# Products of 576 tokens moved as 512 and 64 columns in place of 288 and 288

## The chip, the cores and the metric

The kernel runs on one core of a Trainium2 chip. Its time is the device time of that core in microseconds. The kernel before takes 2556.81 us, the median of two runs (2554.54 and 2559.07).

## The reference

One inference step of a trunk of two layers with a model width of 1024, for 512 prompt tokens and 8 x 8 sample tokens. The kernel takes all 576 tokens through the weights together. Layer 0 has an HGRN2 mixer (a gated linear recurrence with 8 heads), layer 1 an S5 mixer (a diagonal complex state-space layer). Each mixer stands between two half-step SwiGLU feed-forward networks of inner width 2816. All is float32.

```python
def _swiglu(h, w_in, w_out):
    a, b = jnp.split(h @ w_in, 2, axis=-1)
    return (jax.nn.silu(a) * b) @ w_out

for i in range(DEPTH):                                   # DEPTH = 2
    x = x + 0.5 * _swiglu(_rmsnorm(x, ln_ffn1[i]), ffn1_w_in[i], ffn1_w_out[i])
    h = _rmsnorm(x, ln_mix[i])
    out = hgrn2(h) if i == 0 else s5(h)                  # h @ w_in (4 x 1024), ... ; z @ w_glu (2 x 1024)
    x = x + out
    x = x + 0.5 * _swiglu(_rmsnorm(x, ln_ffn2[i]), ffn2_w_in[i], ffn2_w_out[i])
```

## The kernel before

Activations lie with channels on the 128 partitions and the T = 576 tokens along the free axis. The large products run on TensorE in the type fp32r. To keep float32 accuracy each operand is split into a high and a low part, and each product is the sum of three: weights high x activations high, high x low, low x high (w_hi, w_lo; h_hi, h_lo, and likewise g, z, o). A 128x128 block of weights is the stationary operand, the tokens are the moving one.

`product` (line 1655 on) makes one output tile of 128 channels x 576 tokens. It loops over the kt blocks of input channels, over the three part products, and over two halves h of the tokens, HALF = 288 columns each; every half is one matmul, recorded on line 1672, into its own PSUM bank of 512 floats (bank 2s + h, columns 0 to 287). Both halves use the same weights block one after the other. Each matmul call brings its own weight load. Two slots s of two banks each alternate; the semaphore `full[s]` tells that a tile is finished (it is raised by the last matmul of the tile) and `free[s]` that its reader has taken it.

The phases run in order: for each feed-forward network two groups of "up" (kt = 8) and "down" (kt = 12 or 10), the HGRN input and output projections (kt = 8), and the S5 output product "glu" (kt = 8). In the HGRN phase, pieces of a product (a few k) are put between the score levels of the head before (line 1807 and its neighbours), in an order written out by hand. The S5 recurrence has no product beside it except for the first pieces of "glu".

The readers of the PSUM tiles see the two halves through `pair(s)`, a view of two banks with 288 columns each, and bring the SBUF side into the same shape with `halves`. They are `scaled` (line 1086: multiply by the norm's factor), the residual update of "down" (line 1356), and for "glu" the sigmoid on ScalarE (line 1030) and the multiplication on VectorE (line 1614). Other uses of 288-column halves (the sums over channels on lines 1655 and 1863, and the readers of lines 770, 888, 967 and 1600) are not touched. Weights come by DMA into w_raw, ScalarE makes w_hi from them (line 732) and GpSimd w_lo (line 635).

Of the kernel before, what the change touches and what calls it, by code (L numbers as in the profile page):

```python
# [20 lines left out]
ALU = mybir.AluOpType  # L21
ACT = mybir.ActivationFunctionType

D_MODEL = 1024
SEQ = 512
# [10 lines left out]
P = 128  # L36
SAMPLE = DEC_BATCH * DEC_SEQ
T = SEQ + SAMPLE
HALF = T // 2
# [79 lines left out]
def build_trunk(nc, x_prompt, x_sample, state_hgrn, state_s5_re, state_s5_im, ln_ffn1, ffn1_w_in, ffn1_w_out,  # L119
# [9 lines left out]
    def sb(name, shape, dt=F32, at=None):  # L129

        size = 1 if dt == U8 else 4
        for n in shape[1:]:
            size *= n
        size += -size % 32
        where = place["at"] if at is None else at
        if at is None:
            place["at"] += size
        assert where + size <= limit, (name, where + size, limit)
        return nc.alloc_sbuf_tensor_at(name, shape, dt, offset=where)

    x = sb("x", [P, NK, T])
# [6 lines left out]
    rstd = sb("rstd", [P, T])  # L148
# [20 lines left out]
    t_a = sb("t_a", [P, T])  # L169
    t_b = sb("t_b", [P, T])  # L170
    t_s = sb("t_s", [P, T])
# [91 lines left out]
    ps = nc.alloc_psum_tensor("ps", [P, 8, BANK], F32)  # L263
# [9 lines left out]
    def sem(name):  # L273
        return ctx.enter_context(nc.semaphore(name))

    with ctx:
# [13 lines left out]
        free = [sem(f"free{s}") for s in range(2)]  # L290
# [99 lines left out]
        up_at, at = {}, 0  # L390
# [18 lines left out]
        def cols(t, i, n=1):  # L409

            flat = t[:].rearrange("p a b -> p (a b)")
            w = t.shape[2]
            return flat[:, bass.ds(i * w, n * w)]

        def halves(ap):
            return ap.rearrange("p (h t) -> p h t", h=2)

        def pair(s):
            return ps[:, 2 * s:2 * s + 2, 0:HALF]

        def f32(ap):
            return ap.bitcast(F32)

        def lifted(ap):

            return ap.rearrange("p (n t) -> p t n", t=LIFT)
# [280 lines left out]
        def _(act):  # L707
# [26 lines left out]
            def split_next(n, ph, j, i, last):  # L734

                if j == 0:
                    if isinstance(i, int) and i == 0:

                        if n and ph.kind != "hgrn_out":
                            split(ph, 1, 0, PH[n - 1], None)  # L740
                    else:
                        split(ph, 1, i, ph, i - 1)
                elif not last:
                    split(ph, 0, i + 1, ph, i)
                elif n + 1 < len(PH) and (ph.kind, ph.name) not in MAKES:
                    split(PH[n + 1], 0, 0, ph, None)

            def split_ahead(n, ph, j, last):

                if last and j == 0 and n + 1 < len(PH) and (ph.kind, ph.name) in MAKES:  # L750
                    split(PH[n + 1], 0, 0, ph, None)
# [184 lines left out]
            def s5(n, ph):  # L936
# [3 lines left out]
                for q in range(2):  # L940
                    v = ps[:, 6, 2 * P * q:2 * P * (q + 1)].rearrange("p (b s) -> p b s", s=ST)
                    ins = nc.scalar.activation(s5_s[:, q, :, PROMPT_BLOCKS:].rearrange("p s b -> p b s"), v, ACT.Copy)
# [7 lines left out]
                for at in range(NK + 2):  # L950
                    if at < NK:
# [5 lines left out]
                        for h in range(2):  # L957
                            v = ps[0:BLOCKS, h, :].rearrange("n (t g c) -> n t g c", g=G_CT, c=GROUP_CH)
                            ins = nc.scalar.activation(o[:, 4 * h:4 * h + 4], v, ACT.Copy)
# [65 lines left out]
                def unit(i, j, last=False):  # L1025
                    split_next(n, ph, j, i, last)
                    t = i * 2 + (ph.tile0 + j)
                    act.wait_ge(full[1], t + 1)
                    act.wait_ge(gs_done, i * 2 + j)
                    nc.scalar.activation(halves(t_s[:]), pair(1), ACT.Sigmoid).then_inc(free[1], 1)  # L1030
                    split_ahead(n, ph, j, last)
                    norm_tile(5, i * 2 + j, (gs_done, i * 2 + (j + 1)))

                for j in range(2):
                    unit(0, j)
# [6 lines left out]
            for n, ph in enumerate(PH):  # L1042
# [4 lines left out]
                                 scale=1.0 / D_MODEL, bias=eps_t[0:SAMPLE]).then_inc(rms_root, 1)  # L1047
# [10 lines left out]
        def _(dve):  # L1058
            link = Chain(dve, dve_link)
            V = nc.vector  # L1060
# [12 lines left out]
            def clear_ssq(r):  # L1073
                if r:
                    dve.wait_ge(norm_full, r)
                V.memset(ssq[:], 0.0).then_inc(ssq_zero, 1)
                dve.wait_ge(ssq_zero, r + 1)
# [5 lines left out]

            def scaled(dst, s):

                return V.tensor_tensor(halves(dst), pair(s), halves(rstd[:]), ALU.mult)  # L1086


            clear_ssq(0)
            for m in range(NK + 1):  # L1090
                if m < NK:
                    b = 4 + 2 * (m % 2)
# [248 lines left out]
            def down(ph):  # L1341
                r = MAKES.get((ph.kind, ph.name))
                pieces = ph.kind == "down" and ph.name[0] == "ffn1_0"
                if r is not None:
                    if ph.kind == "hgrn_out":
                        dve.wait_ge(o_ready, HEADS)
                    clear_ssq(r)
                scale = 1.0 if ph.kind == "hgrn_out" else 0.5

                def unit(i, j):  # L1350
                    if pieces and j == 0:
                        b_part(i + ph.name[1] * (NK // 2))
                        c_part(i + ph.name[1] * (NK // 2))
                    m = i * 2 + j
                    dve.wait_ge(full[j], i + (ph.tile0 + 1))
                    V.scalar_tensor_tensor(out=halves(cols(x, m)), in0=pair(j), scalar=scale, in1=halves(cols(x, m)),  # L1356
                                           op0=ALU.mult, op1=ALU.add).then_inc(free[j], 1)
                    if r is not None:
                        norm_tile(r, m)

                link.settle()
                at, per = link.base, 6 + 2 + 5 + 5 if pieces else 0
                if pieces:
                    for j in range(2):
                        unit(0, j)
                    assert link.n == per
                    link.n = 0
                with dve.Fori(int(pieces), ph.pairs) as i:
                    link.base = i * per + at
                    for j in range(2):  # L1370
                        unit(i, j)
                    assert link.n == per
                    link.n = 0
                link.base = at + ph.pairs * per
# [163 lines left out]
            def s5(ph):  # L1538
                reciprocal(4)
                for ct in range(NK):  # L1540
                    V.scalar_tensor_tensor(out=u_t[:, ct].rearrange("p (t n) -> p t n", t=LIFT), in0=lifted(x[:, ct]),
                                           scalar=vec[:, NORMS[4][0] + ct:NORMS[4][0] + ct + 1], in1=lifted(rstd[:]),
# [52 lines left out]
                for ct in range(NK):  # L1595

                    dve.wait_ge(t3_full, ct + 1)
                    if ct >= 2:
                        dve.wait_ge(gelu_done, ct - 1)
                    V.scalar_tensor_tensor(out=halves(y_f[ct % 2][:]), in0=halves(u_t[:, ct]),  # L1600
                                           scalar=vec[:, COL["s5_d"] + ct:COL["s5_d"] + ct + 1],
                                           in1=pair(1), op0=ALU.mult, op1=ALU.add).then_inc(yy_done, 1)
# [6 lines left out]
                def unit(i, j):  # L1609
                    t = i * 2 + (ph.tile0 + j)  # L1610
                    m = i * 2 + j
                    dve.wait_ge(full[0], t + 1)
                    dve.wait_ge(free[1], t + 1)
                    V.tensor_tensor(halves(t_a[:]), pair(0), halves(t_s[:]), ALU.mult).then_inc(free[0], 1)
                    dve.wait_ge(free[0], t + 1)
                    V.tensor_tensor(cols(x, m), cols(x, m), t_a[:], ALU.add).then_inc(gs_done, 1)
                    norm_tile(5, m)
# [19 lines left out]
        def _(pe):  # L1637
            M = nc.tensor

            def turn(out, t, n=P, w=P):  # L1640

                return M.transpose(out, t, ident[0:n, 0:n])  # L1642
# [15 lines left out]
            def product(ph, j, a, i, hi, lo, before=None, part=None):  # L1658


                k0, k1 = part or (0, ph.kt)
                s, t = (a, i * 2 + (ph.tile0 + j)) if ph.cols == 2 else (j, i + ph.tile0)
                if k0 == 0:
                    pe.wait_ge(w_ready[j], i + (ph.pair0 + 1))
                    pe.wait_ge(free[s], t)
                for k in range(k0, k1):
                    if before is not None:
                        before(k)
                    at = (a * ph.kt + k) * P
                    for n, (w, v) in enumerate(((w_hi, hi), (w_hi, lo), (w_lo, hi))):  # L1670
                        for h in range(2):
                            ins = M.matmul(ps[:, 2 * s + h, 0:HALF], w[j][:, at:at + P], v[:, k, h * HALF:(h + 1) * HALF],  # L1672
                                           start=k == 0 and n == 0, stop=k == ph.kt - 1 and n == 2)
                if k1 == ph.kt:
                    ins.then_inc(full[s], 1)
# [363 lines left out]
            for c in range(CHUNKS + 1):  # L2039
# [13 lines left out]
                for k in range(NK):  # L2053
                    ins = turn(ps[0:n, Y_BANK[c] + k // 4, (k % 4) * P:(k % 4 + 1) * P], y_n[:, k, c * P:c * P + n])
# [29 lines left out]
```

## Time and profile before

| | |
|---|---|
| two runs | 2554.54 and 2559.07 us |
| median | 2556.81 us |
| span of the profiled execution (no other time is given for it) | 2558.5 us |
| instructions | 42966 |
| TensorE busy | 2370.1 us (93%) |
| TensorE weight loads busy | 2321.2 us (91%) |
| VectorE, ScalarE, GpSimd busy | 1001.8, 664.1, 782.2 us |
| DMA | 211.04 MB, 82 GB/s on average |
| mean granted TensorE clock | 0.961 of full |

Busy times are unions of the instructions' records. A record of a matmul lasts from its start to its modelled end and contains the time in which the result runs through the array, so that consecutive records overlap: how fast they follow each other is read from their starts, or from the number of records in a stretch. An f32 matmul shows as two records, an fp32r matmul as one.

### The profile page before, as it was taken

The numbers are of one execution on the slowest core, as the hardware profiler recorded it, in microseconds if no ns is written. First come the engines' busy times: TensorE is split into PE (matmuls) and PEld (weight loads), VectorE is DVE, ScalarE is ACT, GpSimd is POOL, SyncE is SP. The second block draws the span as 40 slices with busy tenths as digits, with TensorE's granted clock in tenths as the row PEclk, the third lists the DMA queues.
The fourth block names the chain that finished last, engine by engine and source line by source line (L and its number), as shares of the span: only waits on it lengthen the run. The fifth ranks groups of instructions, "written<-read, shape, count | busy, mean of one in ns | idle before, by whom it ended". The sixth has DMA issues, their size and how long they took to land.

```text
span 2558.5 us, 42966 instructions
## 1 busy us (share of the span) xinstructions
PE 2370.1 (93%) x17438; PEld 2321.2 (91%) x17438; DVE 1001.8 (39%) x1538; ACT 664.1 (26%) x750; POOL 782.2 (31%) x223
## 2 busy tenths in 40 slices
PE   6989999998888888999999999999982899999998
PEld 5989999888788877999999999999972899999998
DVE  5845523756665663321122322112259323211222
ACT  3222222332222212322122322122241532221223
POOL 2332333222212212333333333333320133333332
PEclk9999999999898997999999999999986899999999
DMA  4223422441113102432332322232242333223212
GB/s 121 66 61 110 129 82 62 125 112 51 51 50 84 50 17 68 124 90 74 105 102 68 97 82 74 77 96 76 72 136 66 88 82 83 82 70 94 82 58 78
DMA packets 398491, 211.04 MB, mean 82 GB/s; under 512 B 23025, under 2 KB 393922, under 8 KB 398402
## 3 DMA queue, kind: packets, MB, share of 16 engines
q1 hardware_dynamic: 387666, 198.03, 27.9%
q10 hardware_dynamic: 10736, 11.77, 1.4%
q8 instruction: 63, 1.03, 0.2%
q14 instruction: 26, 0.21, 0.0%
HBM read 193.01 MB, written 20.94 MB: 84 GB/s over the span
## 4 chain that ended last, share of the span: by engine, by line
PE 57%; DVE 2%; issue 1%; ACT 1%; POOL 0%; DMA 0%; SPq 0%; DVEq 0%; ACTq 0%
PE ps L1672 55%; PE ps L1642 1%; PE ps L1971 0%; PE ps L1972 0%; DVE sq L1558 0%; DVE sq L1555 0%; DVE ssq L1556 0%; PE ps L1945 0%; POOL w_lo L635 0%; DMA wc<-wc_d 0%; DVE z_lo L1592 0%; DVE s_s L1559 0%; PE ps L1655 0%; DVE s_e L1559 0%; SPq L514 0%
## 5 line engine op out<-in xcount | busy, mean ns | idle before, releaser
L635 POOL TENSOR_TENSOR w_lo<-w_raw,w_hi 128x2048 fp32r<-128x2048 f32 (+3 forms) x184 | 741.6, 4030 | 1584.3 <-ACT w_hi L732 1584.3
L1672 PE MATMUL ps<-h_hi,w_hi 128*128 128x288 f32 x3328 | 731.6, 302 | 17.9 <-DVE t_a L1086 15.6
L1672 PE MATMUL ps<-h_lo,w_hi 128*128 128x288 f32 x3328 | 720.3, 298 | 0.0
L1672 PE MATMUL ps<-h_hi,w_lo 128*128 128x288 f32 x3328 | 719.7, 298 | 0.0
L1672 PEld LDWEIGHTS ps<-h_hi,w_hi 128*128 128x128 f32 x3328 | 544.0, 192 | 23.6 <-DVE t_a L1086 12.7
L1672 PEld LDWEIGHTS ps<-h_lo,w_hi 128*128 128x128 f32 x3328 | 544.1, 191 | 0.0
L1672 PEld LDWEIGHTS ps<-h_hi,w_lo 128*128 128x128 f32 x3328 | 543.7, 191 | 0.0
L732 ACT ACTIVATE w_hi<-w_raw 128x2048 fp32r<-128x2048 f32 (+3 forms) x184 | 309.5, 1682 | 216.5 <-PE ps L1672 204.2
L1672 PE MATMUL ps<-g_hi,w_hi 128*128 128x288 f32 x1408 | 304.7, 298 | 1.4 <-POOL w_lo L635 1.4
L1672 PE MATMUL ps<-g_lo,w_hi 128*128 128x288 f32 x1408 | 302.9, 297 | 0.0
L1672 PE MATMUL ps<-g_hi,w_lo 128*128 128x288 f32 x1408 | 302.7, 297 | 0.0
L1086 DVE TENSOR_TENSOR t_b<-ps,rstd 128x576 f32<-128x576 f32 x88 | 66.6, 757 | 447.2 <-PE ps L1672 447.2
L1672 PEld LDWEIGHTS ps<-g_hi,w_hi 128*128 128x128 f32 x1408 | 228.3, 190 | 1.8 <-issue 1.8
L1672 PEld LDWEIGHTS ps<-g_lo,w_hi 128*128 128x128 f32 x1408 | 228.5, 190 | 0.0
L1672 PEld LDWEIGHTS ps<-g_hi,w_lo 128*128 128x128 f32 x1408 | 228.2, 190 | 0.0
L798 ACT ACTIVATE g_hi<-t_g 128x576 f32 (+1 forms) x88 | 60.4, 686 | 539.7 <-DVE t_g L1314 539.7
L1356 DVE SCALAR_TENSOR_TENSOR x<-ps,x 128x576 f32 (+1 forms) x72 | 54.4, 756 | 360.4 <-PE ps L1672 360.4
L1086 DVE TENSOR_TENSOR t_a<-ps,rstd 128x576 f32<-128x576 f32 x88 | 66.7, 758 | 252.2 <-PE ps L1672 251.3
L795 ACT ACTIVATE t_s<-t_a 128x576 f32<-128x576 f32 x88 | 60.4, 686 | 322.9 <-DVE t_a L1086 322.9
L1807 PE MATMUL ps<-q_t,k_t 128*128 128x128 f32 x512 | 76.3, 297 | 44.3 <-DVE e_t L1403 35.0
L1807 PEld LDWEIGHTS ps<-q_t,k_t 128*128 128x128 f32 x512 | 69.5, 208 | 48.0 <-DVE e_t L1403 37.0
L1316 DVE TENSOR_TENSOR g_lo<-t_g,g_hi 128x576 f32 (+1 forms) x88 | 66.7, 758 | 82.1 <-ACT g_hi L798 82.1
(301 smaller groups left out, 1975.3 us busy)
## 6 DMA issues: line engine op xcount, KB each, us to landing
w_raw<-in_ffn_w_in_dram SPq DMA_DIRECT2D x176, 512.0 KB, 4.9
w_raw<-in_ffn_w_out_dram SPq DMA_DIRECT2D x64, 384.0 KB, 3.7
w_raw<-in_ffn_w_out_dram SPq DMA_DIRECT2D x64, 320.0 KB, 3.4
w_raw<-in_hgrn_w_in_dram SPq DMA_DIRECT2D x32, 512.0 KB, 5.3
w_raw<-in_s_w_glu_dram SPq DMA_DIRECT2D x16, 512.0 KB, 4.7
wb_d<-wb_st ACTq DMA_DIRECT2D x8, 512.0 KB, 2.8
wc_d<-c_pow ACTq DMA_DIRECT2D x8, 512.0 KB, 3.5
s_in<-in_state_hgrn_dram SPq DMA_DIRECT2D x8, 512.0 KB, 4.0
```

The lines of the kernel that those rows point to most:

```text
L635: nc.gpsimd.tensor_tensor(w_lo[j][:, 0:n], w_raw[j][:, 0:n], f32(w_hi[j][:, 0:n]), ALU.subtract)\
L732: nc.scalar.activation(w_hi[j][:, 0:ph.size], w_raw[j][:, 0:ph.size], ACT.Copy).then_inc(w_hi_done[j], 1)
L795: nc.scalar.activation(t_s[:], t_a[:], ACT.Silu).then_inc(silu_done, 1)
L798: nc.scalar.activation(cols(g_hi, i * 2 + j), t_g[:], ACT.Copy).then_inc(g_hi_done, 1)
L1086: return V.tensor_tensor(halves(dst), pair(s), halves(rstd[:]), ALU.mult)
L1316: V.tensor_tensor(cols(g_lo, i * 2 + j), t_g[:], f32(cols(g_hi, i * 2 + j)), ALU.subtract)\
L1356: V.scalar_tensor_tensor(out=halves(cols(x, m)), in0=pair(j), scalar=scale, in1=halves(cols(x, m)), op0=ALU.mult, op1=ALU.add).then_inc(fr ...
L1642: return M.transpose(out, t, ident[0:n, 0:n])
L1672: ins = M.matmul(ps[:, 2 * s + h, 0:HALF], w[j][:, at:at + P], v[:, k, h * HALF:(h + 1) * HALF], start=k == 0 and n == 0, stop=k == ph.kt ...
L1807: ins = M.matmul(ps[:, 4 + n % 2, at], k_t[b][:, at], q_t[b][:, at], start=True, stop=True)
```

## The change

Line 1672 moves tokens 0 to 511 in one matmul of 512 columns, which fills bank 2s, and tokens 512 to 575 in one of 64 columns into the start of bank 2s + 1. The number of matmuls and of weight loads, their order and their semaphores stay. A tile then lies contiguous over the two banks, and a new view `both(s)` gives its 576 columns in one piece to the four readers, which read and write plain 576-element rows (the fifth edited place is the new view itself).

```diff
@@ -418,6 +418,10 @@
         def pair(s):
             return ps[:, 2 * s:2 * s + 2, 0:HALF]
 
+        def both(s):
+
+            return ps[:, 2 * s:2 * s + 2, :].rearrange("p b t -> p (b t)")[:, 0:T]
+
@@ -1027,7 +1031,7 @@
-                    nc.scalar.activation(halves(t_s[:]), pair(1), ACT.Sigmoid).then_inc(free[1], 1)
+                    nc.scalar.activation(t_s[:], both(1), ACT.Sigmoid).then_inc(free[1], 1)
@@ -1083,7 +1087,7 @@
-                return V.tensor_tensor(halves(dst), pair(s), halves(rstd[:]), ALU.mult)
+                return V.tensor_tensor(dst, both(s), rstd[:], ALU.mult)
@@ -1353,7 +1357,7 @@
-                    V.scalar_tensor_tensor(out=halves(cols(x, m)), in0=pair(j), scalar=scale, in1=halves(cols(x, m)),
+                    V.scalar_tensor_tensor(out=cols(x, m), in0=both(j), scalar=scale, in1=cols(x, m),
                                            op0=ALU.mult, op1=ALU.add).then_inc(free[j], 1)
@@ -1611,7 +1615,7 @@
-                    V.tensor_tensor(halves(t_a[:]), pair(0), halves(t_s[:]), ALU.mult).then_inc(free[0], 1)
+                    V.tensor_tensor(t_a[:], both(0), t_s[:], ALU.mult).then_inc(free[0], 1)
@@ -1668,8 +1672,8 @@
                     for n, (w, v) in enumerate(((w_hi, hi), (w_hi, lo), (w_lo, hi))):
-                        for h in range(2):
-                            ins = M.matmul(ps[:, 2 * s + h, 0:HALF], w[j][:, at:at + P], v[:, k, h * HALF:(h + 1) * HALF],
+                        for h, (t0, t1) in enumerate(((0, SEQ), (SEQ, T))):
+                            ins = M.matmul(ps[:, 2 * s + h, 0:t1 - t0], w[j][:, at:at + P], v[:, k, t0:t1],
                                            start=k == 0 and n == 0, stop=k == ph.kt - 1 and n == 2)
```

## Rows read from the trace of the kernel before

**Rows 1.** The page: engines (busy us, share, instructions) and the granted clock in 40 slices.

```profile
PE 2370.1 (93%) x17438; PEld 2321.2 (91%) x17438; DVE 1001.8 (39%) x1538; ACT 664.1 (26%) x750; POOL 782.2 (31%) x223
...
PEclk9999999999898997999999999999986899999999
```

**Rows 2.** TensorE's waits: who for whom, us in total, times, longest.

```profile
PE ps L1807 <- DVE e_t L1403: 35.0, 9, 4.7
PE ps L1807 <- DVE q_t L1386: 9.3, 7, 2.5
PE ps L1672 <- DVE z_lo L1592: 5.0, 6, 2.0
```

**Rows 3.** Stretches: length, busy us (xcount) by engine, clock, DMA; the first, line 1672 alone.

```profile
540.00:1000.00 460.00, 256.31 (x1618) 237.04 (x1618) 0.90 0.18 51
...
1200.00:1300.00 100.00, 100.00 (x753) 100.00 (x752) 12.61 (x17) 18.33 (x14) 35.87 (x9) 1.00 0.38 104
1860.00:2010.00 150.00, 88.82 (x836) 82.80 (x835) 104.06 (x208) 59.82 (x101) 15.31 (x10) 0.78 0.38 109
```

**Rows 4.** Groups of TensorE on line 1672, one of three: xcount, busy us, mean ns.

```profile
L1672 PE MATMUL ps<-h_hi,w_hi 128*128 128x288 f32 x3328 | 731.6, 302 | 17.9 <-DVE t_a L1086 15.6 <-issue 2.0 <-POOL w_lo L635 0.3
...
L1672 PE MATMUL ps<-g_hi,w_hi 128*128 128x288 f32 x1408 | 304.7, 298 | 1.4 <-POOL w_lo L635 1.4
...
L1672 PE MATMUL ps<-z_hi,w_hi 128*128 128x288 f32 x256 | 56.7, 304 | 5.9 <-DVE z_lo L1592 5.0 <-ACT t_s L1030 0.8
...
L1672 PE MATMUL ps<-o_hi,w_hi 128*128 128x288 f32 x128 | 31.4, 330 | 9.0 <-DVE o_lo L1474 4.6 <-POOL w_lo L635 4.4
```

**Rows 5.** Timeline of TensorE, 8-column products: start us, us, instruction.

```profile
660.49 1.95 PE L1856 MATMUL ps<-q_t,s_in 128*128 128x8 f32 x16
```

**Rows 6.** Timeline of TensorE, 128-column products, and the record lengths of their neighbours.

```profile
653.89 1.05 PE L1834 MATMUL ps<-v_tok,k_tok 128*128 128x128 f32 x8
...
L1834 PE MATMUL ps<-v_tok,k_tok 128*128 128x128 f32 x64 | 9.5, 295 | 0.8 <-ACT k_tok L879 0.8
```

**Rows 7.** Records of loads, and the 8-column product: duration ns min/median/max.

```profile
L1672 PEld LDWEIGHTS ps<-h_hi,w_hi x3328: 186/188/338, 27.2 to 2479.1; 128*128 128x128 f32 x196
...
L1856 PEld LDWEIGHTS ps<-q_t,s_in x128: 186/192/333, 606.6 to 970.3; 128*128 128x128 f32 x128
L1856 PE MATMUL ps<-q_t,s_in x128: 256/256/380, 606.6 to 970.4; 128*128 128x8 f32 x128
```

**Rows 8.** Timeline of the weight loads and products of line 1842, 512 columns.

```profile
656.46 0.29 PEld L1842 LDWEIGHTS ps<-v_seq,k_tok 64*128 64x128 f32 x2 [0.17 <-issue]
657.00 0.19 PEld L1842 LDWEIGHTS ps<-v_seq,k_tok 64*128 64x128 f32 x1 [0.24 <-issue]
657.43 0.19 PEld L1842 LDWEIGHTS ps<-v_seq,k_tok 64*128 64x128 f32 x1 [0.24 <-issue]
...
656.46 1.98 PE L1842 MATMUL ps<-v_seq,k_tok 64*128 64x512 f32 x4
```

**Rows 9.** Timeline of TensorE at the half clock.

```profile
861.49 0.68 PE L1672 MATMUL ps<-h_hi,w_lo 128*128 128x288 f32 x2
861.97 0.68 PE L1672 MATMUL ps<-h_hi,w_hi 128*128 128x288 f32 x2
```

**Rows 10.** Timeline of TensorE, f32 products of 288 columns, and their record length.

```profile
1035.15 1.13 PE L1655 MATMUL ps<-ssq,ones 128*128 128x288 f32 x4
...
L1655 PE MATMUL ps<-ssq,ones x24: 404/406/511, 41.4 to 2126.9; 128*128 128x288 f32 x24
```

**Rows 11.** The page, groups: a reader of PSUM and the making of w_lo.

```profile
L1086 DVE TENSOR_TENSOR t_b<-ps,rstd 128x576 f32<-128x576 f32 x88 | 66.6, 757 | 447.2 <-PE ps L1672 447.2
...
L635 POOL TENSOR_TENSOR w_lo<-w_raw,w_hi 128x2048 fp32r<-128x2048 f32 (+3 forms) x184 | 741.6, 4030 | 1584.3 <-ACT w_hi L732 1584.3
```

## Prediction

> **What bounds the kernel now.** I read the page's busy times first: TensorE is busy 93% of the span and its weight loads 91%, at a granted clock that is full in most slices [rows 1]. Then the waits of TensorE: the longest is 35.0 us in total [rows 2], so hardly anything but its own stream holds it. Then the stretches: from 1200 to 1300 us it issues 753 products and is never idle, while VectorE is busy 12.61 us of 100 [rows 3]. The groups of instructions say which stream that is. Line 1672 has 3 x (3328 + 1408 + 256 + 128) = 15,360 matmuls of 288 columns, 7,680 pairs [rows 4]. Per pair the dense stretch gives 2 x 100 / 753 = 0.2656 us, so 7,680 pairs are 2,040 us of the 2,558.5 us span. This change touches exactly that stream: whatever a pair gains or loses lies on the path that sets the end.
>
> **What a matmul is made of.** Every matmul, the second with the same weights too, has a weight load of its own: 753 loads and products in the dense stretch [rows 3]. What the load takes has to be read from stretches where the product is too short to hide it. The 8-column products of line 1856 carry 128x128 weights: sixteen last 1.95 us of which the last's own record is 0.256, so they follow at (1.95 - 0.256) / 15 = 0.113 us [rows 5], though 8 columns are next to no work. The eight 128-column products of line 1834 follow at (1.05 - 0.295) / 7 = 0.108 us [rows 6]. So one load costs 0.108 to 0.113 us however short its product is. That those are f32 and ours fp32r makes no difference in the load's record: 188 ns for line 1672, 192 for line 1856 [rows 7].
> How far ahead can a load run? Line 1842 has 512 columns in each record: the third and fourth loads start at 657.00 and 657.43, one product apart, after 0.24 us in which the load side stood idle [rows 8]. So with 0.43 us of room, loads do not run two ahead: the next starts when the product before it does. A pair of 288s hides both loads (two products of 0.133 against loads of 0.11). In 512 + 64 the load for the 64 hides under the 512, but the load for the next 512 can start only with the 64, whose columns are over long before.
>
> **The change, part by part.**
> *The 512-column product.* At the half clock the 288 columns take 0.24 us (two products from 861.49 to 861.97) [rows 9], one column per cycle of 1.2 GHz, so at 2.4 GHz they are 0.120 and the 0.1328 measured holds 0.0128 more. 512 columns are 0.2133. Lower bound: the 288-column f32 products of line 1655 follow at (1.13 - 0.406) / 3 = 0.241 us, twice 0.120 and about 0.001 more [rows 10], so the excess might vanish: 0.215. Upper bound: the excess grows with the columns, 0.1328 x 512 / 288 = 0.236. I take it as a fixed sum per product, 0.226, the middle between them.
> *The 64-column product.* 64 columns are 0.027 us, the load behind it 0.108 to 0.113. The load decides; I take 0.113, as the 8-column rows are nearest to a short product.
> *The pair.* 0.226 + 0.113 = 0.339 us in place of 0.2656: +0.0734. Bounds 0.323 and 0.349: +0.057 and +0.083. Over 7,680 pairs: **+564 us**, bounds +440 and +641.
> *Pairs at the half clock.* From 540 to 1000 us, 1,618 matmuls of line 1672 are busy 256.3 us [rows 3] against 1,618 x 0.1328 = 215; of the 41 us over, I put 15 to the tails of separate pieces (9 steps of some 10 pieces by the code, 0.16 us each), so 26 / 0.107, about 240 matmuls or 120 pairs, ran at 1.2 GHz. There the pair would go from 0.480 to 0.427 + 0.217 (twice the fast load) = 0.644, 0.09 more than the 0.073 counted: +10 us.
> *Waits that a slower TensorE fills.* In the HGRN stage the products lie between the score levels; a longer piece covers the 9.3 us for VectorE's q_t [rows 2] and perhaps the few us for z_lo in the S5 stage. The 35.0 us for e_t are 9 waits; a piece of three k ahead of each is 9 pairs and grows by 0.7 us, so some 6 us go and the rest stays. Together -18 us.
> *The five readers of PSUM.* They read the same 576 elements, contiguous rather than two times 288; VectorE's take 757 ns and have 447.2 us of idle time behind TensorE [rows 11]. Cost nothing; if a record became 50 ns longer or shorter, only the last of each stage would reach the end, under 1 us. No queue, wait, DMA or semaphore moves. Weight supply gets more time: GpSimd's 184 groups busy 741.6 us, behind ScalarE 1584.3 us idle [rows 11].
> **Sum:** 564 + 10 - 18 = +556. The page gives no time of its own for the profiled execution beyond the span, 2558.5; it lies between the two runs (2554.54 and 2559.07), 1.7 above their median 2556.81. 2556.81 + 556 = **3113 us**, 22% slower.
>
> **Rivals.**
> *Two loads ahead, or the second load of the same weights for nothing.* Then the 64 costs its columns and one overhead, 0.028 to 0.040, and the pair 0.243 to 0.266: between -0.0226 x 7,680 = -174 us and no change; its middle 0.255 gives -82, 2475 us. It decides from the point at which the short product's cost falls under 0.040. For it: nothing in the rows shows fp32r loads behind a short fp32r product. Against: rows 5 and 8. By the Trainium skill, "TensorE: Matmul & The Clock Gate", section "Back-to-back issue gap", 512 columns are 518 cycles and 1 to 64 columns about 60; a pair would be 578 / 2.4 = 241 ns, and the time about 2370, faster. The trace speaks against that table for streams with a weight load each (8 columns: 113 ns, not 25), and its 134 cycles (56 ns) for 128 columns aren't met either (108 ns). Chance 0.03: two thirds faster, one third within 2%.
> *Load and short product one after the other.* If the load for the next 512 began only once the 64 columns are through, 0.027 is added: +205, 3325 us. For it: 0.113 against 0.108 could be that. Against: the 128-column products at 0.108, whose columns alone take nearly that, leave no room for a load in series [rows 6]. Or fp32r could run narrow products at a slower rate; up to four cycles a column (the rate of the two f32 records) 64 columns are 0.107 and still hidden by the load, so it costs only in series, +0.107 x 7,680 = +820. Chance 0.07, mostly near 3325.
> *The narrow product is taken in two passes as f32 is.* Two records with a load each: +0.113 more, +868, 3990 us. The f32 groups show such doubling (line 1842: four records for two products) [rows 8], fp32r at 288 columns none. Chance 0.03.
> *The clock falls.* TensorE's columns fill 0.240 of 0.339 us, 71%, in place of 90%. In the S5 stretch it was busy 89 of 150 us and the granted clock 0.78 [rows 3], but with idle stretches in it, which this stream hasn't. If everything ran at 1.2 GHz the pair were 0.644: +2,900, 5460 us. Chance 0.03.
> Forecast 0.84.
>
> **Numbers.** The forecast's own bounds are 2557 + 440 - 18 = 2979 and 2557 + 641 + 10 = 3208, the lower only if both ends of a pair fall low together. The range goes to 3000 and 3260: it takes in most of the forecast's 0.84 and hardly any of the rest; 0.8 in all. 2% is about what a measurement of this kernel can tell from no change. Faster by over 2%: 0.02, within 2%: 0.01, slower: 0.97.
>
> **What would show it.** In the dense stretches a 512-column and a 64-column product in turn, some 590 products per 100 us in place of 753; from the start of a 64 to the next 512 about 0.11 us, from the start of a 512 to its 64 about 0.22 to 0.23; the load side idle about 0.1 us in each pair; the granted clock still 1.0 there; VectorE's and ScalarE's busy times as before, their idle time longer; the wait for q_t gone. Wrong if the step from 64 to 512 takes 0.04 or less, if 0.14 or more, or if the records of the 64s are twice as many.

## The result

The changed kernel takes 3098.05 us (3096.75 to 3099.35) beside 2556.81 before: ratio 1.2107, 95% interval 1.2085 to 1.213. The forecast was 3113 us in a range of 3000 to 3260. Its profiled execution has a span of 3095.0 us, 536.5 more than before.

The page of the changed kernel, engines and granted clock (against [rows 1]):

```profile
span 3095.0 us, 42966 instructions
...
PE 2949.6 (95%) x17438; PEld 2569.8 (83%) x17438; DVE 989.4 (32%) x1538; ACT 663.4 (21%) x750; POOL 777.9 (25%) x223
...
PEclk9999999999989979999999999999977999999999
```

As many instructions, the other engines as busy as before, and TensorE alone longer. The load side fell from 91% of the span to 83%: it now stands idle in every pair. A dense stretch of the changed kernel (length, busy us with xcount of PE, PEld, DVE, ACT, POOL, granted clock, DMA share, GB/s; against the row of 1200 to 1300 in [rows 3]):

```profile
1500.00:1600.00 100.00, 100.00 (x587) 87.48 (x585) 18.20 (x24) 19.06 (x18) 27.49 (x6) 1.00 0.28 75
```

587 products in place of 753, at full clock and with no idle time: a pair is 200 / 587 = 0.3407 us, 0.0751 more. A record counts in every stretch that it touches, so a short stretch counts two or three products too many. A longer one of each kernel, the changed one first, then the one before, one fence each:

```profile
1500.00:2000.00 500.00, 500.00 (x2923) 437.25 (x2921) 93.38 (x115) 97.51 (x95) 138.34 (x35) 1.00 0.24 66
```

```profile
1200.00:1800.00 600.00, 600.00 (x4499) 599.79 (x4498) 129.35 (x163) 142.69 (x133) 216.34 (x53) 1.00 0.31 87
```

So the better figures are 1000 / 2923 = 0.3421 us a pair beside 1200 / 4499 = 0.2667, 0.0754 more. Some of the timeline of the changed kernel; first the weight loads, then what is under way at 1500.50:

```profile
1500.34 0.30 PEld L1676 LDWEIGHTS ps<-h_lo,w_hi 128*128 128x128 f32 x2
1500.68 0.30 PEld L1676 LDWEIGHTS ps<-h_hi,w_lo 128*128 128x128 f32 x2
...
1500.33 0.19 PE L1676 MATMUL ps<-h_hi,w_hi 128*128 128x64 f32 x1
...
1500.36 0.48 PE L1676 MATMUL ps<-h_lo,w_hi 128*128 128x512 f32 x1
```

Each PEld row is two loads, and repeats after 0.34 us. A load's record is 0.19 long (median 190 ns), so the second load of a row starts 0.30 - 0.19 = 0.11 after the first. The first belongs to the 512 and starts with the 64-column product (1500.33 and 1500.34). The second belongs to the next 64, and starts when the first load is through, at about 1500.45; I take it that the 512 columns begin to move then. No further load starts until the next 64 does, 0.23 us later; of these, the load's own record covers 0.19, and 0.04 us of each pair show as idle. The PE rows alone would mislead: the record of the 512 starts 0.03 us after that of the 64 and contains the wait for its load.

The readers of PSUM in the changed kernel, against [rows 11]:

```profile
L1090 DVE TENSOR_TENSOR t_b<-ps,rstd 128x576 f32<-128x576 f32 x88 | 66.7, 758 | 606.0 <-PE ps L1676 606.0
L639 POOL TENSOR_TENSOR w_lo<-w_raw,w_hi 128x2048 fp32r<-128x2048 f32 (+3 forms) x184 | 737.7, 4009 | 2098.9 <-ACT w_hi L736 2098.9
```

758 ns in place of 757 for the contiguous read, and 159 us more of waiting for TensorE. TensorE's own waits in the changed kernel, against [rows 2] and, of the kernel before, the row for b_pow, which stands first here:

```profile
PE ps L1642 <- DVE b_pow L1260: 15.6, 8, 4.7
```

```profile
PE ps L1811 <- DVE e_t L1407: 25.2, 9, 3.5
...
PE ps L1676 <- DVE z_lo L1596: 4.3, 4, 2.0
PE ps L1646 <- DVE b_pow L1264: 4.0, 4, 2.5
...
PE ps L1811 <- DVE q_t L1390: 2.0, 3, 1.1
```

### The profile page after: what moved, and what is told of

Read it like the earlier page. It is cut to its first block, busy times and chain, and to the rows that moved or that the text cites. A ratio compares the mean times of both kernels' runs of the same rounds, so it can differ in the third digit from the quotient of the medians.

```text
span 3095.0 us, 42966 instructions
## 1 busy us (share of the span) xinstructions
PE 2949.6 (95%) x17438; PEld 2569.8 (83%) x17438; DVE 989.4 (32%) x1538; ACT 663.4 (21%) x750; POOL 777.9 (25%) x223
## 4 chain that ended last, share of the span: by engine, by line
PE 60%; DVE 2%; issue 1%; ACT 0%; DMA 0%; SPq 0%; POOL 0%; DVEq 0%; ACTq 0%
PE ps L1676 59%; PE ps L1646 1%; PE ps L1975 0%; PE ps L1976 0%; DVE sq L1562 0%; DVE sq L1559 0%; DVE ssq L1560 0%; PE ps L1949 0%; DMA wc<-wc_d 0%; DVE z_lo L1596 0%; SPq L518 0%; PE ps L1659 0%; DVE s_s L1563 0%; DVE s_e L1563 0%; DVE rstd L1085 0%
## 5 line engine op out<-in xcount | busy, mean ns | idle before, releaser
L1676 PE MATMUL ps<-h_hi,w_hi 128*128 128x512 f32 (+1 forms) x3328 | 854.2, 338 | 8.6 <-DVE t_a L1090 6.7
L1676 PE MATMUL ps<-h_lo,w_hi 128*128 128x512 f32 (+1 forms) x3328 | 854.3, 338 | 0.0
L1676 PE MATMUL ps<-h_hi,w_lo 128*128 128x512 f32 (+1 forms) x3328 | 843.6, 335 | 0.0
L1676 PEld LDWEIGHTS ps<-h_hi,w_hi 128*128 128x128 f32 x3328 | 506.9, 192 | 80.2 <-issue 6.1
L1676 PEld LDWEIGHTS ps<-h_hi,w_lo 128*128 128x128 f32 x3328 | 502.8, 191 | 76.7
L1676 PEld LDWEIGHTS ps<-h_lo,w_hi 128*128 128x128 f32 x3328 | 505.9, 192 | 71.2
L1676 PE MATMUL ps<-g_lo,w_hi 128*128 128x512 f32 (+1 forms) x1408 | 358.0, 335 | 0.0
L1676 PE MATMUL ps<-g_hi,w_hi 128*128 128x512 f32 (+1 forms) x1408 | 356.9, 335 | 0.0
L1676 PE MATMUL ps<-g_hi,w_lo 128*128 128x512 f32 (+1 forms) x1408 | 353.3, 332 | 0.0
L1676 PEld LDWEIGHTS ps<-g_hi,w_lo 128*128 128x128 f32 x1408 | 210.2, 189 | 32.0
L1811 PE MATMUL ps<-q_t,k_t 128*128 128x128 f32 x512 | 77.6, 298 | 27.3 <-DVE e_t L1407 25.2
```

What stands on the lines that cost most here:

```text
L1676: ins = M.matmul(ps[:, 2 * s + h, 0:t1 - t0], w[j][:, at:at + P], v[:, k, t0:t1], start=k == 0 and n == 0, stop=k == ph.kt - 1 and n == 2)
L1811: ins = M.matmul(ps[:, 4 + n % 2, at], k_t[b][:, at], q_t[b][:, at], start=True, stop=True)
```

## The experiments

My theory: the whole loss is a weight load of 0.11 us that shows behind every short product. All experiments go by three numbers: the count of products in a dense stretch, the step between the loads, and the granted clock. Some kernels leave out a part of the large products, as the text ahead of each says; of those the times alone are of use. "The changed kernel" is the one with 512 and 64 columns.

**Other widths.** The first part ends at the end of bank 2s, so that the 576 columns stay contiguous for the readers (N1 = 288, 320, 384, 448):

```diff
-                        for h, (t0, t1) in enumerate(((0, SEQ), (SEQ, T))):
-                            ins = M.matmul(ps[:, 2 * s + h, 0:t1 - t0], w[j][:, at:at + P], v[:, k, t0:t1],
+                        for h, (t0, t1) in enumerate(((0, N1), (N1, T))):
+                            c0 = (BANK - N1) * (1 - h)
+                            ins = M.matmul(ps[:, 2 * s + h, c0:c0 + t1 - t0], w[j][:, at:at + P], v[:, k, t0:t1],
...
-            return ps[:, 2 * s:2 * s + 2, :].rearrange("p b t -> p (b t)")[:, 0:T]
+            return ps[:, 2 * s:2 * s + 2, :].rearrange("p b t -> p (b t)")[:, BANK - N1:BANK - N1 + T]
```

> Two products of 288 columns again, but laid contiguously across the border of the two banks (columns 224 to 511 of the first, 0 to 287 of the second), with the four readers contiguous as in the changed kernel: the readers' part of the change alone. My theory (all of the +541 us is the weight load that shows behind the short product, the readers cost nothing): as the kernel before, 2550 to 2563 us, a pair 0.2656 us. Rival (the contiguous reads across a bank border cost or gain something): off by more than 5 us.

Measured: 2558.34 us, ratio 0.9999 (0.999 to 1.0008). The readers, contiguous across a bank border, cost and gain nothing; the whole loss is in the widths.

> 320 and 256 columns. Theory (a pair costs the long product at about 0.438 ns per column plus 0.007, and the short one the larger of its own columns and a load of 0.110): 0.147 + 0.119 = 0.266 us, 2557 us. Rival (narrow products of fp32r run slower per column, from some width below 288 on): slower than 2600.

Measured: 2558.8 us, ratio 1.0001 (0.9992 to 1.0011). 256 columns still cover a load.

> 384 and 192 columns. Theory (load hides the columns of the short product or is hidden by them): 0.175 + 0.110 = 0.285 us a pair, 3098 - 7680 x 0.056 = 2670 us. Rival A (a narrow fp32r product takes four cycles a column, 0.320 us here): 0.495 us, 4280 us. Rival B (0.083 of load after 0.0267 of columns, one after the other, which gives the same 0.110 at 64 columns): 0.175 + 0.080 + 0.083 = 0.338, 3080 us.

Measured: 2697.92 us, ratio 1.0546 (1.0527 to 1.0565).

> 448 and 128 columns. Theory: 0.203 + 0.110 = 0.313 us a pair, 2885 us. Rival A (four cycles a column): 0.203 + 0.213 = 0.416, 3680 us. Rival B (columns and load one after the other): 0.203 + 0.053 + 0.083 = 0.339, 3085 us.

Measured: 2886.23 us, ratio 1.1282 (1.1261 to 1.1303). A dense stretch of each of the three kernels, 320, 384 and 448 in this order, one fence each (columns as above):

```profile
1250.00:1350.00 100.00, 100.00 (x752) 100.00 (x751) 21.23 (x28) 22.52 (x22) 36.98 (x8) 1.00 0.40 104
```

```profile
1250.00:1350.00 100.00, 100.00 (x692) 100.00 (x691) 11.36 (x15) 16.84 (x13) 34.93 (x9) 1.00 0.34 92
```

```profile
1250.00:1350.00 100.00, 100.00 (x641) 95.54 (x640) 14.40 (x19) 17.11 (x15) 30.10 (x8) 1.00 0.22 63
```

The pair is 0.266, 0.289, 0.312 us, and 0.3407 with 512. The loads of 384/192, then those of 448/128; the second of a row again starts 0.30 - 0.19 = 0.11 after the first:

```profile
1500.20 0.30 PEld L1677 LDWEIGHTS ps<-g_hi,w_hi 128*128 128x128 f32 x2
1500.49 0.30 PEld L1677 LDWEIGHTS ps<-g_lo,w_hi 128*128 128x128 f32 x2
```

```profile
1300.29 0.30 PEld L1677 LDWEIGHTS ps<-g_hi,w_lo 128*128 128x128 f32 x2
1300.61 0.30 PEld L1677 LDWEIGHTS ps<-g_hi,w_hi 128*128 128x128 f32 x2
```

So the step behind the short product is 0.11 us for 64, 128 and 192 columns alike (0.109 by the starts of all loads in these stretches), and what is left for the long one is its columns and some 0.016 to 0.02: both rivals, a slow rate of narrow products and load and columns in series, are out. 448/128 came out within 2 us of the theory, 384/192 28 us above it, 0.004 us a pair; why the one and not the other is open.

**Which load shows.** Half of the weight columns for the wide (H = 0) or the narrow product (H = 1):

```diff
+                            m = P // 2 if h == H and (k or n) and not (k == ph.kt - 1 and n == 2) else P
-                            ins = M.matmul(ps[:, 2 * s + h, 0:t1 - t0], w[j][:, at:at + P], v[:, k, t0:t1],
+                            ins = M.matmul(ps[0:m, 2 * s + h, 0:t1 - t0], w[j][:, at:at + m], v[:, k, t0:t1],
```

> 512 and 64 columns, but the 512-column product takes only 64 of the block's 128 weight columns, except in the first and the last of a tile (so half of the output channels miss most of their sum for the prompt tokens). The moved columns stay. Theory (what shows is the load of the NEXT product, the wide one, behind the 64 columns): the load falls by the 0.054 us by which a record of a 64-column load is shorter (132 against 186 ns); 7680 x 0.93 x 0.054 = 385 us less, 2715 us. Rival (the 64-column product is slow by itself, 0.11 us whatever is loaded): 3098 us.

Measured: 2767.75 us, ratio 1.0814 (1.0783 to 1.0846). The two loads of a pair in this kernel:

```profile
1520.15 0.25 PEld L1677 LDWEIGHTS ps<-g_lo,w_hi 128*64 128x64 f32 x2
1520.45 0.25 PEld L1677 LDWEIGHTS ps<-g_hi,w_lo 128*64 128x64 f32 x2
```

The second, of 128 weight columns and 0.19 long, starts 0.25 - 0.19 = 0.06 after the first in place of 0.11. Of the 385 us expected 330 came: the load behind the short product gave back what it should, but the step of the wide product grew by about 0.005 us (3369 products from 1300 to 1800 us, a pair 0.297), some 38 of the 55 missing, and no run shows why.

> The same with the 64-column product: it takes 64 of the 128 weight columns, except in the first and the last of a tile (half of the output channels miss most of their sum for the sample tokens). Theory: its load lies under the 512 columns before it and is hidden, so nothing changes: 3098 us. Rival (the product's own load or own array work is the cost): 2715 us.

Measured: 3113.24 us, ratio 1.2164 (1.2129 to 1.22), half a per cent above the changed kernel and 400 us away from the rival. The load that shows is that of the wide product behind the narrow one. The narrow product's own is hidden. The 15 us above the changed kernel stand in the dense stretch too (from 1500 to 1600 us 582 products in place of 587) and are not explained.

**Each product by itself.**

```diff
+                            if h != KEPT and (k or n):
+                                continue
...
-                                           start=k == 0 and n == 0, stop=k == ph.kt - 1 and n == 2)
+                                           start=k == 0 and n == 0, stop=h != KEPT or (k == ph.kt - 1 and n == 2))
```

KEPT is 0 in the first of the two kernels and 1 in the second.

> The 64-column product is made only for the first part product of a tile and left out for the others (the sample tokens miss most of their sum), so that 512s follow each other. Theory: each pair loses 0.110 us, 7680 x 0.965 x 0.110 = 815, so 2285 us; the 512s follow at 0.231 us, which is between my fixed excess (0.226, 2245 us) and an excess that grows with the columns (0.236, 2320 us). Rival (the 512-column product itself became slow, and the 64 costs 0.03): 2860 us or more, 512s at 0.31.

Measured: 2337.77 us, ratio 0.9134 (0.9077 to 0.9192). Its dense stretch:

```profile
1500.00:1600.00 100.00, 100.00 (x449) 82.77 (x448) 17.43 (x23) 23.20 (x19) 42.84 (x11) 1.00 0.35 97
```

With one 64 in about 25 to 37 products (some 15 of the 449, at 0.11), a 512 takes (100 - 15 x 0.11) / 434 = 0.2266 us: an excess of 0.013 over its columns (512 / 2.4 = 213 ns), as for 288 columns. So in a stream without gaps the excess is a sum per product and doesn't grow with the columns. The time is 53 us above the estimate. Waits of TensorE that longer products had covered are back: it is idle for 2329.9 - 2114.6 = 215 us in place of 145. Two of them are 23.3 us for b_pow (4.0 in the changed kernel) and 39.1 for e_t (25.2), in this kernel's list of waits:

```profile
PE ps L1813 <- DVE e_t L1407: 39.1, 10, 5.3
...
PE ps L1646 <- DVE b_pow L1264: 23.3, 8, 5.8
```

> The 512-column product is made only for the first part product of a tile and left out for the others (the prompt tokens miss most of their sum), so that 64s follow each other. Theory: they follow at the pace of the load, 0.109 to 0.113 us, in stretches where nothing else holds TensorE; time 1390 us and more, since other engines become the bound. Rival (64 columns with a load cost 0.03 when the queue is full of them): 0.03 to 0.05 us apart.

Measured: 2386.52 us, ratio 0.9325 (0.9298 to 0.9352), far above what I had expected. Its granted clock in 40 slices, and its weight loads:

```profile
PEclk9998555655555556555555555555557755555555
```

```profile
1520.09 0.33 PEld L1678 LDWEIGHTS ps<-h_lo,w_hi 128*128 128x128 f32 x1
1520.30 0.33 PEld L1678 LDWEIGHTS ps<-h_hi,w_lo 128*128 128x128 f32 x1
```

```profile
180.20 0.33 PEld L1678 LDWEIGHTS ps<-h_hi,w_lo 128*128 128x128 f32 x1
180.41 0.33 PEld L1678 LDWEIGHTS ps<-h_hi,w_hi 128*128 128x128 f32 x1
```

TensorE, never idle in that stretch (1500 to 1600 us: 100.00 busy at 0.50), got 1.2 GHz in place of 2.4, and the 64s follow at 0.213 us, twice 0.107. The first digits of the clock row, 9998, don't contradict that: the first clock record of this profile is at 219 us, the row reads full where there is none, and the loads at 180 us are as far apart as those at 1520. The load does set the pace, but of a clock that I hadn't foreseen.

**The excess, the order, and narrower still.** The same halving of the weight columns for both products, on the 288/288 kernel:

> 288 and 288 columns as before, but all products take only 64 of the 128 weight columns, except in the first and the last part product of a tile (half of the output channels miss most of their sum). Question: what is the 0.0128 us that each product takes over its 288 columns? Theory A (it is the product's own and has nothing to do with the load under it): 2558 us. Theory B (it is the disturbance by the load's reads): it falls to about 0.001 to 0.007, so 80 to 170 us less, 2390 to 2480 us.

Measured: 2536.33 us, ratio 0.9912 (0.9896 to 0.9929). In the 380 dense us from 1250 to 1440 and from 2200 to 2390 it made 2888 products where the kernel before makes 2853 (the counts of the two stretches less one each), 0.1316 in place of 0.1332 us. Nine tenths of the excess stay: Theory A but for a tenth. Half the weight columns are also half the outputs, so the tenth need not be the load's.

```diff
-                    for n, (w, v) in enumerate(((w_hi, hi), (w_hi, lo), (w_lo, hi))):
-                        for h, (t0, t1) in enumerate(((0, SEQ), (SEQ, T))):
+                    for h, (t0, t1) in enumerate(((0, SEQ), (SEQ, T))):
+                        for n, (w, v) in enumerate(((w_hi, hi), (w_hi, lo), (w_lo, hi))):
```

> The changed kernel, in other order: for each block k the three 512-column part products and then the three 64-column ones. Theory (each 64-column product costs the load of whatever comes behind it, 0.109 us, in any order): 3098 us. Rival (the cost is one of switching from a long to a short product and back, or between banks): two of three switches are gone, 2560 to 2740 us. A third thing, seen with the 64s alone: three in a row might lower the granted clock, then slower than 3098.

Measured: 3103.21 us, ratio 1.2141 (1.2119 to 1.2163): the changed kernel's time within 5 us, and the same 587 products in a dense stretch of 100 us. The order is worth nothing; each short product leaves one load open wherever it stands.

```diff
+                            if h and (k or n) and not (k == ph.kt - 1 and n == 2):
+                                t1 -= SAMPLE // 2
```

> 512 and 32 columns (half of the sample tokens are left out of all part products but the first and last of a tile). Theory (the load sets the cost of the short product, its columns count for nothing): 3098 us. Rival (load and columns one after the other): 0.0133 us less a pair, 7680 x 0.93 x 0.0133 = 95, 3003 us.

Measured: 3419.95 us, ratio 1.3364 (1.3338 to 1.339). Half the work of the short product made the kernel 322 us slower. Its granted clock, two short stretches and a long one:

```profile
PEclk8555699999998885899999999999977557999999
```

```profile
1360.00:1380.00 20.00, 20.00 (x65) 16.92 (x63) 5.83 (x3) 3.15 (x3) 4.55 (x1) 0.50 0.39 97
...
1400.00:1420.00 20.00, 20.00 (x119) 17.54 (x118) 4.68 (x6) 3.86 (x4) 4.58 (x1) 1.00 0.24 63
```

```profile
1500.00:2000.00 500.00, 500.00 (x2927) 437.66 (x2926) 91.00 (x112) 96.38 (x94) 138.25 (x35) 1.00 0.25 69
```

All three are the same stream without a gap. At full clock it makes 2927 products in 500 us, where the changed kernel makes 2923: that the columns of the short product count for next to nothing holds. But this stream stays at 1.2 GHz from its start to 400 us (but for 7 us at 56), from 1278 to 1397 at the end of the HGRN stage and from 2616 to 2868 behind the S5 stage. The changed kernel first gets 2.4 GHz at 36 us, and none of its later half-clock stretches lasts over 31 us. A pair at 1.2 GHz, from one row to the next:

```profile
355.11 0.80 PE L1678 MATMUL ps<-h_hi,w_hi 128*128 128x512 f32 x2
355.75 0.80 PE L1678 MATMUL ps<-h_lo,w_hi 128*128 128x512 f32 x2
```

The mean clock is 0.872 beside 0.969. At two levels only, that makes 2 x (1 - 0.872) x 3418 = 875 us at 1.2 GHz beside 2 x (1 - 0.969) x 3095 = 192, so 683 us more. A pair takes 0.64 us there in place of 0.342, which loses 47% of them, some 318 us: the difference, by this estimate.

> 384 and 192 columns, the 384-column product made only for the first part product of a tile (the first 384 tokens miss most of their sum), so that 192s follow each other, with the columns 0.080 of the load's 0.109 us (73%, as in the 512 and 64 stream). With 64s alone the granted clock fell to 0.50 and they followed at 0.213 us. Theory A (the clock follows how much of the time columns move): near 1.0 in the feed-forward stretches, 192s at 0.109 to 0.112 us. Theory B (any stream in which the load is the bound gets half the clock): 0.50 and 0.213 us, near 2390 us.

Measured: 1959.54 us, ratio 0.7659 (0.7642 to 0.7677). A stretch of its feed-forward part:

```profile
1350.00:1450.00 100.00, 79.23 (x554) 77.36 (x552) 42.08 (x43) 33.87 (x35) 53.99 (x15) 0.85 0.42 116
```

The clock is 0.85, and TensorE waits 21% of the time for others. It goes back and forth between the two levels within this stretch: the loads follow at 0.11 us in one place and at 0.21 in the next.

```profile
1350.02 0.19 PEld L1679 LDWEIGHTS ps<-h_hi,w_hi 128*128 128x128 f32 x1
1350.13 0.19 PEld L1679 LDWEIGHTS ps<-h_lo,w_hi 128*128 128x128 f32 x1
```

```profile
1356.06 0.33 PEld L1679 LDWEIGHTS ps<-h_lo,w_hi 128*128 128x128 f32 x1
1356.27 0.33 PEld L1679 LDWEIGHTS ps<-h_hi,w_lo 128*128 128x128 f32 x1
```

The load sets the pace at both, so theory B is out. The clock is nearer to theory A, but not 1.0, so how it is granted is left open.

No version that makes all the products beats the kernel before: 288/288 and 320/256 are equal, every other split that was run is slower.

## Why the prediction was right

- *The bound.* The 7,680 pairs on line 1672 set the time: 7,680 x 0.0754 = 579 us from the long dense stretches, and the span grew by 536.5.
- *The load behind the 64.* Predicted from the 8-column rows at 0.113, it is 0.109 by the step of the loads, for 64, 128 and 192 columns; shown by halving it (to 0.06, 330 us less) and by halving the wrong one (nothing gained).
- *The 512.* Taken at 0.226; by itself it takes 0.2266. In the pair 0.3421 - 0.109 = 0.233 are left for it. So the load was put 0.004 too high and the 512 0.007 too low, and the two mostly cancel: 0.339 forecast, 0.342 measured. Against the pair before, +0.0734 was forecast and +0.0754 came, 15 us in all. Halving the weight columns in e9 took a tenth of the excess away, so reads of the load may be a part; the rest isn't explained.
- *No load two ahead.* The argument from the 512-column records held: in each pair no load starts while the 512 moves, until the next 64 starts. The load side shows idle for 0.04 us a pair and not the 0.1 forecast, since its records last 0.19 where the loads follow at 0.109.
- *The table of the rival.* By the Trainium skill, "TensorE: Matmul & The Clock Gate", section "Back-to-back issue gap", that table is the gap of an isolated matmul, which leaves out the load and so "under-counts" at few columns; the prediction took it for a stream with a load at each product. The 241 ns that it gives a pair are not met here: 342 were measured.
- *The waits that a slower TensorE fills.* Forecast 18 us, and this is the term that was too small: TensorE's idle time fell from 2558.5 - 2370.1 = 188.4 us to 3095.0 - 2949.6 = 145.4, by 43. I had counted q_t (9.3 to 2.0) and a part of e_t (35.0 to 25.2), and overlooked b_pow in the preparation of the S5 matrices between "down" tiles (15.6 to 4.0), and t_a (15.6 to 6.7). 579 - 43 = 536, beside the 536.5.
- *Half-clock pairs.* Forecast +10 us on the assumption that they stay as many, and that a pair goes from 0.480 to 0.644. The second held: the first pairs of the changed kernel, at half clock, are 0.64 us apart (28.06 and 28.70). The first didn't: by the clock records of the two traces 291 products of the line start at half clock before and 218 after, some 146 and 109 pairs. They cost 146 x (0.480 - 0.267) = 31 us more than at full clock before, 109 x (0.64 - 0.342) = 32 after; the term is about 1 us.
- *Luck.* The pairs brought 15 us more than forecast, the waits took 25 more and the half clock brought 9 less. That the forecast of +556 stands only 15 us over the +541 of the medians owes something to errors that go against each other, in the pair (load and 512) and between the pair and the waits. The 3325 and 3990 us given for two rivals should be 3318 and 3981 by their own sums.
- *The readers.* Nothing, shown by 288/288 in the contiguous layout. There are four of them, not five as the text said.
- *A test that I wrote wrongly.* "Wrong if the step from 64 to 512 takes 0.04 or less" goes by the records of the products, and these start 0.03 us apart, though the mechanism is right. The step of the loads is the one to read.
- *The clock.* The rival had 0.03. It didn't come, but it stood closer than I thought: 32 columns fewer and a quarter of the run is at half clock.

## What to carry to other kernels

A short matmul is worth its columns only if they last as long as the weight load behind it, 0.11 us here for 128 weight columns of fp32r at full clock: 256 moved columns covered it, 192 did not, and nothing between them was run. If 576 columns have to go in two pieces, halve them: 320 and 256 cost nothing, and each split from 384 and 192 on cost about what its short product lacks. To judge a stream, count products over some hundred us (a short stretch counts the records at its edges too) and look at the steps of the loads; a product's record can contain the wait for its load.

## What the runs showed of the hardware that I had not expected

A stream of TensorE that is not idle can be granted half the clock. 64-column products alone ran at 0.50 through nearly the whole kernel. The stream of 512 and 32 columns stayed at 0.50 for nearly all of the first 400 us and for 120 and 250 us behind the two later gaps, though the same stream ran at 1.00 for hundreds of us in between. With 64 in place of 32 no such stretch was over 31 us. So less array work under the same loads cost 322 us; what decides it, no run here shows. And the excess of a product over its columns is 0.013 us for 288 and 512 columns alike where every load is hidden, and 0.016 to 0.02 for the long product of a pair whose other load shows.
